# The first block's output product, taken in parts that follow the three mixers, and ScalarE's first wait

## What is computed

```python
hn = rms_norm(h, norm1_g[i])
z = hn @ w_in[i]
ya = rms_norm(stick_breaking_attention(...), sb_out_g[i])
hb = rms_norm(mlstm_chunkwise(...), mnorm_g[i])       # per head
yb = hb * jax.nn.sigmoid(ob)
yc = rms_norm(spatial_gating(...), sgu_out_g[i])
h = h + jnp.concatenate([ya, yb, yc], axis=-1) @ w_out[i]
h = h + hierarchical_moe(rms_norm(h, norm2_g[i]), ...)
```

## Time and profile before

| | us |
|---|---|
| median of 3 runs | 1434.82 |
| the runs | 1430.45, 1438.96, 1434.82 |
| profiled execution, own time | 1433.19 |
| its span, first to last instruction | 1431.4 |

### The profile page before, as it was taken

The page is one execution under the profiler, slowest core; times in us unless marked ns, Lnnn a source line. Parts: engine busy times, 40 slices in busy tenths (PEclk is TensorE's granted clock), DMA queues, the critical chain, the costliest instruction groups (busy, mean ns, idle before and its releaser), DMA issues.

```text
span 1431.4 us, 22554 instructions
## 1 busy us (share of the span) xinstructions
PE 1236.1 (86%) x8265; PEld 665.8 (47%) x8265; DVE 534.0 (37%) x1574; ACT 257.7 (18%) x527; POOL 25.2 (2%) x126
## 2 busy tenths in 40 slices
PE   6999978787566666999998897996999999999966
PEld 4763254544223232874444444653455445544523
DVE  0002531643111212499964634532333433343323
ACT  2113421211000122201045412110111111111100
POOL 1000110000000000000000001000000000000000
PEclk9999959799778868899999998998999999999987
DMA  8447940889999768054431441679899999999992
GB/s 296 162 176 290 394 153 0 313 352 378 421 421 421 300 230 303 1 200 176 153 118 59 162 185 65 250 303 426 356 384 410 396 398 398 390 408 403 392 420 114
DMA packets 87568, 400.04 MB, mean 279 GB/s; under 512 B 10944, under 2 KB 19620, under 8 KB 58800
## 3 DMA queue, kind: packets, MB, share of 16 engines
q1 hardware_dynamic: 86272, 398.15, 70.6%
q10 hardware_dynamic: 816, 0.52, 0.1%
q0 software_dynamic: 384, 0.03, 0.0%
HBM read 397.60 MB, written 1.07 MB: 279 GB/s over the span
## 4 chain that ended last, share of the span: by engine, by line
PE 48%; DMA 5%; ACT 2%; DVE 2%; issue 1%; PEld 1%; PEldq 0%; ACTq 0%; DVEq 0%; SPq 0%
PE ps L2132 16%; PE ps L411 13%; PE ps L441 7%; PE ps L377 5%; PE ps L386 3%; DMA big<-in_w_exp_down 2%; PE ps L2169 2%; DMA ring<-in_w_exp_gu 2%; PE ps L367 1%; PE ps L430 1%; ACT big L891 0%; DVE big L1928 0%; DVE big L1930 0%; ACT parts L873 0%; PE ps L913 0%
## 5 line engine op out<-in xcount | busy, mean ns | idle before, releaser
L411 PE MATMUL ps<-ring,big 128*32 128x512 f32 x2144 | 281.8, 616 | 67.7 <-DMA ring<-in_w_up 45.7
L411 PEld LDWEIGHTS ps<-ring,big 128*32 128x32 f32 x2144 | 81.8, 114 | 228.6 <-issue 228.6
L441 PE MATMUL ps<-big 128*32 128x512 f32 x1216 | 141.3, 606 | 13.5 <-DMA big<-in_w_exp_down 6.8
L2132 PE MATMUL ps<-ring,big 128*128 128x512 f32 x320 | 138.0, 593 | 1.6 <-ACTq L885 1.1
L411 PE MATMUL ps<-big 128*32 128x512 f32 x288 | 121.0, 624 | 10.9 <-DMA ring<-in_w_exp_gu 9.7
L377 PEld LDWEIGHTS ps<-big 128*128 128x128 bf16 x1920 | 113.7, 98 | 32.7 <-issue 30.2
L377 PE MATMUL ps<-big 128*128 128x128 bf16 x1920 | 123.6, 220 | 1.4 <-ACT big L264 1.4
L1916 DVE SCALAR_TENSOR_TENSOR big<-big 128x256 f32<-128x256 f32 x240 | 105.6, 481 | 8.9
L340 DVE TENSOR_TENSOR big<-big,ps 128x256 f32<-128x256 f32 x38 | 16.0, 421 | 237.4 <-ACT big L272 237.2
L2132 PEld LDWEIGHTS ps<-ring,big 128*128 128x128 f32 x320 | 60.6, 190 | 77.2 <-issue 75.1
L386 PE MATMUL ps<-parts,slot_tok 128*128 128x512 f32 x304 | 82.9, 416 | 8.8 <-issue 5.2
(11 more groups left out here) (451 smaller groups left out, 1259.4 us busy)
## 6 DMA issues: line engine op xcount, KB each, us to landing
ring<-in_w_exp_gu SPq DMA_DIRECT2D x55, 2048.0 KB, 12.6
big<-in_w_exp_down SPq DMA_DIRECT2D x64, 1024.0 KB, 9.1
big<-in_w_down SPq DMA_DIRECT2D x32, 1024.0 KB, 18.3
ring<-in_w_in SPq DMA_DIRECT2D x15, 2048.0 KB, 9.3
ring<-in_w_gate SPq DMA_DIRECT2D x28, 1024.0 KB, 18.5
ring<-in_w_up SPq DMA_DIRECT2D x28, 1024.0 KB, 20.6
ring<-in_w_ada SPq DMA_DIRECT2D x12, 2048.0 KB, 8.6
big<-in_w_exp_gu SPq DMA_DIRECT2D x9, 2048.0 KB, 13.1
```

The costliest lines, as they stand in the source:

```text
L411: last = pe.matmul(ps[rows, BG, :], m.xsT[:, k, rows], m.gu(gu[j], k), start=(k == 0), stop=(k == KC - 1), skip_group_check=True)
L441: last = pe.matmul(ps[rows, BD + n, :], m.hidT[:, k, rows], m.dring[:, down[j], k * D + n * 512:k * D + n * 512 + 512], start=(k == 0), st ...
L2132: last = pe.matmul(bank, lhs(k), rhs(k), start=(k == 0 and start), stop=(k == kk - 1))
```

## The change

ScalarE's table preload moves ahead of its waits, and instead of `consts` it waits for `eps_set`, a new increment on GpSimd's drain behind the memset of `eps_c`, and for x.

The output product is cut up by the order in which its chunks come. TensorE transposes the attention's chunks (YA) after the mLSTM products, and, once ScalarE has copied them (`yT_ready` 1), runs k = 0, 1, 2 of three of the four tiles, (0,0), (0,1) and (1,0), into banks 0, 1 and 2. Then come the transposes of the gating (YC) and the mLSTM (YB), k = 6, 7 of the three tiles, their k = 3, 4, 5, and the fourth tile whole. Each transposed chunk has a place `at` in banks 4 to 7, so that those of YA and YC don't touch bank 7, which VectorE still reads. On ScalarE the copies are in three groups around the mLSTM's root. On VectorE the scaling of the gating moves ahead of the mLSTM's squares.

```diff
--- before.py
+++ after.py
@@ -856,6 +856,7 @@
         L_SD = add_load(A["w_sh_down_2"][0].rearrange("(k p) n -> p k n", p=P), 2, D, "sh_d", 1)
         add_moe(m2)
         NUM = (7, 3)
+        YA, YC, YB = ((0, 0), (1, 1), (2, 2)), ((6, 4), (7, 5)), ((3, 3), (4, 6), (5, 7))
 
 
         def load(sp, i):
@@ -998,7 +999,7 @@
                 pool.memset(sel4[:], 0.0)
                 pool.memset(selq[:], 0.0)
                 pool.memset(eps_c[:], EPS)
-                pool.drain()
+                pool.drain().then_inc(ev("eps_set"), 1)
                 pool.affine_select(out=ident[:], in_=ident[:], compare_op=ALU.not_equal, fill=1.0, base=0,
                                    pattern=[[-1, P]], channel_multiplier=1)
                 pool.affine_select(out=ntri[:], in_=ntri[:], compare_op=ALU.is_ge, fill=0.0, base=0,
@@ -1061,8 +1062,8 @@
 
             @first.scalar
             def _(act):
-                act.wait_ge(ev("consts"), 1)
                 act.preload_act_table_set(LOG_EXP)
+                act.wait_ge(ev("eps_set"), 1)
                 act.wait_ge(ev("x_in"), 32)
                 for t in range(TT):
                     act.activation(parts[:, t, :], x_tm[:, t, :], ACT.Square, accum_out=stat[:, t:t + 1])
@@ -1182,17 +1183,23 @@
                             act.activation(parts[:, t, 0:SBW], ps[:, t, 0:SBW], ACT.Square, accum_out=stat[:, 48 + t:49 + t])
                         act.drain()
                         rstd(48, 2, None, "ya_rstd", SBW)
+                def y_out(places, banks_done):
+
+                    for (c, at), done in zip(places, banks_done):
+                        act.wait_ge(ev("y_T"), done)
+                        act.activation(hT[:, c, :], ps[:, 4 + at // 2, (at % 2) * T:(at % 2 + 1) * T], ACT.Copy,
+                                       scale=cols[:, R_YG + c:R_YG + c + 1])
+                    act.drain().then_inc(ev("yT_ready"), 1)
+
                 act.wait_ge(ev("yc_raw"), 1)
                 for t in range(TT):
                     act.activation(parts[:, t, 0:SGW], hn_tm[:, t, SBW + MLW:D], ACT.Square, accum_out=stat[:, 50 + t:51 + t])
                 act.drain()
                 rstd(50, 2, None, "yc_rstd", SGW)
+                y_out(YA, (1, 1, 2))
                 rstd(24, 8, "yb_ss", "yb_rstd", MLD)
-                for c in range(KC):
-                    act.wait_ge(ev("y_T"), c // 2 + 1)
-                    act.activation(hT[:, c, :], ps[:, 4 + c // 2, (c % 2) * T:(c % 2 + 1) * T], ACT.Copy,
-                                   scale=cols[:, R_YG + c:R_YG + c + 1])
-                act.drain().then_inc(ev("yT_ready"), 1)
+                y_out(YC, (3, 3))
+                y_out(YB, (4, 5, 5))
 
 
 
@@ -1339,6 +1346,7 @@
                         dve.wait_ge(ev("ya_rstd"), 1)
                         for t in range(TT):
                             dve.tensor_scalar(ya[:, t, :], ps[:, t, 0:SBW], stat[:, 48 + t:49 + t], None, ALU.mult)
+                        dve.drain().then_inc(ev("ya_ready"), 1)
 
                 dve.wait_ge(ev("sgu_mix"), 1)
                 mixed = ps[:, 2, :].rearrange("p (t g c) -> p t g c", t=TT, g=SGG)
@@ -1367,6 +1375,10 @@
                     dve.tensor_tensor(hb[:, t], num[t][:, :, 0:MLD], den[:, t, :].unsqueeze(2).to_broadcast([P, MLH, MLD]),
                                       ALU.mult)
                 dve.drain()
+                dve.wait_ge(ev("yc_rstd"), 1)
+                for t in range(TT):
+                    dve.tensor_scalar(yc[:, t, :], yc[:, t, :], stat[:, 50 + t:51 + t], None, ALU.mult)
+                dve.drain().then_inc(ev("yc_ready"), 1)
                 for t in range(TT):
                     dve.tensor_tensor(scratch[:, t, 0:MLW], hn_tm[:, t, SBW:SBW + MLW], hn_tm[:, t, SBW:SBW + MLW], ALU.mult)
                 dve.drain()
@@ -1374,9 +1386,6 @@
                     dve.tensor_reduce(stat[:, 24 + 4 * t:28 + 4 * t],
                                       scratch[:, t, 0:MLW].rearrange("p (h d) -> p h d", h=MLH), AX.X, ALU.add)
                 dve.drain().then_inc(ev("yb_ss"), 1)
-                dve.wait_ge(ev("yc_rstd"), 1)
-                for t in range(TT):
-                    dve.tensor_scalar(yc[:, t, :], yc[:, t, :], stat[:, 50 + t:51 + t], None, ALU.mult)
                 dve.wait_ge(ev("yb_rstd"), 1)
                 for t in range(TT):
                     dve.tensor_tensor(hb[:, t], hb[:, t],
@@ -1633,16 +1642,46 @@
                     if h + 2 < MLH:
                         ml_s(h + 2)
 
+                def y_transposes(places):
+
+                    for i, (c, at) in enumerate(places):
+                        for t in range(TT):
+                            last = pe.transpose(ps[:, 4 + at // 2, (at % 2) * T + t * P:(at % 2) * T + (t + 1) * P],
+                                                hn_tm[:, t, c * P:(c + 1) * P], ident[:])
+                        if i + 1 == len(places) or places[i + 1][1] // 2 != at // 2:
+                            last.then_inc(ev("y_T"), 1)
+
+                def out_part(n, t, ks, start, stop):
+
+                    w = loads[L_OUT[n]]["dst"]
+                    for k in ks:
+                        last = pe.matmul(ps[:, 2 * n + t, :], hT[:, k, t * P:(t + 1) * P], w[:, k, :],
+                                         start=(start and k == ks[0]), stop=(stop and k == ks[-1]))
+                    return last
+
+                EARLY = ((0, 0), (0, 1), (1, 0))
+                pe.wait_ge(ev("ya_ready"), 1)
+                y_transposes(YA)
+                pe.wait_ge(ev("yc_raw"), 1)
+                for n in range(2):
+                    arrived(pe, L_OUT[n])
+                pe.wait_ge(ev("yT_ready"), 1)
+                for n, t in EARLY:
+                    out_part(n, t, (0, 1, 2), True, False)
+                pe.wait_ge(ev("yc_ready"), 1)
+                y_transposes(YC)
                 pe.wait_ge(ev("y_ready"), 1)
-                transposes(pe, hn_tm, 4, "y_T")
-                pe.wait_ge(ev("yT_ready"), 1)
+                y_transposes(YB)
+                pe.wait_ge(ev("yT_ready"), 2)
+                for n, t in EARLY:
+                    out_part(n, t, (6, 7), False, False)
+                pe.wait_ge(ev("yT_ready"), 3)
                 for n in range(2):
-                    w = loads[L_OUT[n]]["dst"]
-                    arrived(pe, L_OUT[n])
                     for t in range(TT):
-                        for k in range(KC):
-                            last = pe.matmul(ps[:, 2 * n + t, :], hT[:, k, t * P:(t + 1) * P], w[:, k, :],
-                                             start=(k == 0), stop=(k == KC - 1))
+                        if (n, t) in EARLY:
+                            last = out_part(n, t, (3, 4, 5), False, True)
+                        else:
+                            last = out_part(n, t, tuple(range(KC)), True, True)
                         last.then_inc(ev("o_proj"), 1)
```

## The result

| | before | after |
|---|---|---|
| median, us (4 runs each) | 1435.19 | 1421.05 |
| the runs of after | | 1418.71, 1419.86, 1422.24, 1426.80 |
| ratio, 95% interval | | 0.9909 (0.9881 to 0.9936) |
| profiled execution, span | 1431.4 | 1425.1 |

The ratio says 13.1 us less, between 9.2 and 17.1; the forecast was 9.0 us, as 1425.8 in a range of 1421.7 to 1431.5. The profiled execution of after is the slowest of its four, so its trace shows less of the gain than the median does: 6.3 us between the spans.

A forecast was written before the change was run, and what follows sets the result against it. TensorE is busy nine tenths of most of the span, and the stream bounding the MoE begins when the output product ends. Start 3.5 plus tail 5.5 made 9.0 us, off 1434.8: 1425.8 us, range 1421.7 to 1431.5.

The forecast's parts named there:

- the start: ScalarE's earlier first step makes the gate product 3.5 us earlier, all of it counted through to the end.
- the tail: Mixers' end: output product begun early ends at 243.4 instead of 248.87, 5.5 us won, bounds 4.6 and 7.6.
- signs that it named for being wrong: Wrong if clock stays 0.50 beyond 6 us, MoE's first transfers don't move by 9, or clock changes in untouched stretches.
- x as the next wait: ScalarE's first square, waiting for x, starts at 5.2 instead of 8.73: 3.5 us earlier, bounds 3.3 and 4.1.
- The chain behind it moves as it is.: Reciprocal root, L1228 and transposes behind ScalarE's first square keep their lengths, carrying 3.5 us to the gate product.
- The queue ahead of the norm row: DMA transfers ahead of the gating mixer's norm row (wait 2.4 us, until 190.2) move with the rest, keeping all 3.5.
- rival (a): One half is lost on the way: start swallowed by saturated transfers, 1429.3, or tail by MoE, 1431.3; chance 0.20 together.
- The early product: Output product's first 18 instructions start at 211.9, lose 2.1 us at half clock (bounds 0 and 3), end at 221.8.
- The scaling of the gating, moved: On VectorE, L1379 ahead of the mLSTM squares makes y_ready 0.7 us later, covered by the early product.
- (b): Early product runs wholly at half clock, 15.6 us, and the tail gains nothing: 1431.5; chance 0.05.
- (c): Slower: clock doesn't rise in the output product at all, which ends 21.1 us late: 1452.4; chance 0.04.
- (d): More than forecast: clock is up at the early product, or x lands at once; 11.1 us, 1423.7; chance 0.06.

The follow-up runs named there:

- e1: Kernel before with only the new start (table preload first, eps_set in place of consts), old output product: ratio 0.9991, 1432.45 us.
- e4: The changed kernel timed again, against the kernel before: ratio 0.9920, 1424.03 us.
- e6: Changed kernel with attention chunks transposed after the gating products and 12 of 18 early instructions run between mLSTM products: ratio 0.9934, 1425.99 us.
- e2: Changed kernel with the old first wait, so only the early output product is new: ratio 0.9929, 1423.81 us.
- e11: Kernel before with five spare products in TensorE's idle 7 us ahead of the 16 transposes: ratio 0.9995, 1434.87 us.
- e13: Kernel before, unchanged, traced once more: 1434.84 us.
- e14: Kernel before, unchanged, traced yet another time: 1431.87 us.
- e9: Kernel before with SyncE waiting for the gating mixer's small rows ahead of the first four experts: ratio 0.9923, 1424.55 us.
- e3: Changed kernel with SyncE waiting for the gating mixer's small rows ahead of the first four experts: ratio 0.9855, 1413.50 us.
- e12: e8 plus 14 spare products in TensorE's idle 4 us ahead of the last attention head's correction: ratio 0.9864, 1416.33 us.
- e8: e3 plus two spare products of 512 columns in TensorE's gap ahead of the early product: ratio 0.9868, 1417.14 us.
- e10: e9 plus the start of the change, output product as before: ratio 0.9917, 1424.47 us.

## Why the prediction was right, and where it was not

The forecast had the sign, the places and most of the steps: faster by over half a per cent, the MoE's transfers behind `h1_ready` earlier by what the product is earlier, and the two parts of the product, counted from G, where it put them: 21.7 and 32.7 us behind it, forecast 21.7 and 33.3. The size, 9.0, is just outside the first interval (9.2 to 17.1) and inside the second (7.6 to 15.5). That its sum agrees with that of the marks, 8.8, is luck, since its two terms were wrong in opposite directions: the start was put at 3.5 and gave some 1.6, the tail at 5.5 and gave some 7.2. One of the signs that it named for being wrong did show, a clock that changes in stretches that the edit doesn't touch: ahead of G and in the mLSTM. But it changes there between executions of the kernel before as well.

**x as the next wait.** Right: ScalarE waits for x, from the table load on. Size: 5.64 instead of 5.2, so 3.1 us instead of 3.5, under the lower bound of 3.3.

**"The chain behind it moves as it is."** This step failed. The gate product began 3.1 us earlier with the new start, but mostly took 8.7 to 9.4 us instead of 7.07, and at G the mean is 187.9 in the four traces of the new start with the old queue (after, e1, e4, e6) and 189.5 in the five of the old (before, e2, e11, e13, e14): 1.6 us, with a scatter of 4. e1's 1.3 us in time says the same, within an interval of 5. In the profile of before this product was slow too (9.12 us), and I took that as the kernel's; so its own pair of traces hides the loss, and the many traces show it.

**The queue ahead of the norm row.** I held it to move with the rest, and gave the loss of it a chance in rival (a). The two traces alone looked like rival (a): the wait grew from 2.4 to 3.43. But e13 and e14 show 5.8 and 0.6 in the same kernel, so this wait is a scatter of 5 us that covers what the start wins. That it stands on the path is shown by e9 and e3, which remove it and are faster; G itself comes only 2 to 3 us earlier in them than in these means.

**The early product.** Forecast 9.9 us for 18 instructions with 2.1 lost at the half clock; measured 9.66 twice (after and e4) and 7.96 once (e2; 7.8 is the time without a loss). The reason was right too, with a difference: the clock was not low from the mLSTM on. It rose with its end, fell inside the product after the idle 1.99 us, and rose again 3.4 us later. The 10 transposes took 1.25 us (1.23 forecast), the wait ahead of the rest 0.30 (0.5), and the 46 instructions 20.01 (19.9).

**The gain of the tail.** 5.5 forecast; G to X fell from 58.5, the mean of six traces, to 52.7, 50.8 and 50.5, 7.2 in the mean. The term that was too small is the price of the old order. I charged the old product nothing for the clock, since in the earlier trace rows the rise came just before it; in four of six traces it took 29.8 to 30.1 us, and where it took 27.7, the mLSTM had paid instead. With the new order the second payment is at most the 1.9 us inside the early product, and what the mLSTM gains is kept: in e4, where its last product starts 16.3 us after G, G to X is 50.5, against 58.6 in e14 with the same mLSTM. In the forecast's own case, the slow mLSTM of before and after (18.6), the gain is 6.0, near the 5.5.

**The scaling of the gating, moved.** It cost nothing, as forecast: `y_ready` was there at 215.3 (L1391 and L1394 end), and TensorE asked for it after 219.8.

**Rivals (b), (c) and (d).** Neither (b) nor (c) came: the early product ran at half for 3.4 of its 9.66 us. The argument against (b) misread one thing: the low stretch from 205 to 210 also held products of 256 columns (L1605), not only 64 to 97. The total is nearest to (d), 11.1 us, which had a chance of 0.06, but (d)'s reasons came only in part: the clock was up at the early product in e2, and x did not land at once.

**What stays open.** Start and tail, by marks, are 1.6 + 7.2 = 8.8 us; the two parts timed alone give 1.3 and 10.2; the change gives 13.1 and 11.5. In a stage that the edit doesn't touch, the gated projection's product (L1678, L1717 in the kernel after), the pair of traces differs by 1.3 us, before and after:

```profile
521.08 30.73 PE L1678 MATMUL ps<-ring,big 128*128 128x512 f32 x64 [1.66 <-ACT big L1213]
```
```profile
513.98 29.40 PE L1717 MATMUL ps<-ring,big 128*128 128x512 f32 x64 [2.16 <-ACT big L1220]
```

It is 30.7 or 30.8 in the six traces with the old order and 29.1 to 29.4 in after, e2 and e4; but e11, with the old order, has 29.4, and of the others with the new one e6 and e3 have some 30.7, e12 29.4 and e8 27.7, so the early product isn't its cause. Nor does it reach the end: from X to the end of the span before takes 1182.5 us and after 1183.9. The 3 to 4 us that the times give over the marks lie within the intervals, and no run here tells them from chance.

The rule of the Trainium skill that transposes do not count for the clock ("TensorE: Matmul & The Clock Gate", Part 4) does not hold as it stands for these float32 transposes: before's rise at 220.0 had 3.4 us of nothing but them in front of it, and e13's had all 16 and then 0.4 us of nothing. But what I took from that, that the old product is spared, was too much: in e1, e9, e10 and e14 the same transposes ran their 3.7 us at the half clock, the rise came 4.2 to 4.8 us into the product, and it lost 2.1 to 2.4 us, as the forecast had worked out for that rule.

## What to carry to other kernels

A product that sums over chunks from several sources can be begun with those that are ready, and here it was best spent as cover for the last chain of the others, behind the last work that this chain needs; ahead of that work it delayed the chain (e6, one trace). Before costing a gain at the start or a wait for a small transfer from one trace, look at a second trace of the same kernel: here the same wait was 5.8, 2.4 and 0.6 us. And small transfers whose reader is near should not stand among large ones whose reader is far: one wait on SyncE gave as much as the whole change, though the traces account for only 2 to 3 us of it.

## What the runs showed of the hardware

The granted clock was at 0.50 while TensorE counted as busy for nearly all of the mLSTM (products of 64 to 256 columns), and at 1.00 through the same instructions in e3: from G to the gating's product with u (L1350 of before) the stage took 10.3 us instead of 18.1. The rows ahead of it tell e3 from e8 in one thing, when the clock had come back from its last fall (us, busy PE, clock, DMA share, GB/s), e3 and then e8:

```profile
179.00:180.00 1.00, 1.00 (x9) 0.85 0.98 418
```
```profile
181.00:182.00 1.00, 1.00 (x3) 0.61 1.01 426
```

That is 5.9 us ahead of G in e3 and 4.3 in e8; in e4, e9 and e10 it is 4.3 to 4.4. But in e12 the clock had been up since before 168, and it fell 2.3 us behind G all the same. So what decides it stays open. G to X is 3.7 us shorter in e3 than in e8, although e3 paid 1.7 us in the early product and e8 did not.

An idle stretch of 2.0 to 2.7 us ahead of the early product was followed by a fall to 0.50 inside the product in after, e4 and e3, and by none in e2 (2.53 us).
